# A feed-forward stage on TensorE with its matmuls in another order: the two token halves interleaved, weights shared by neighbours

## What is computed

```python
def reference(x, norm1_gain, w_in, ..., norm2_gain, w_ffn_gate, w_ffn_up, w_ffn_down):
    ...
        h = h + mixed @ w_out[l]
        u = rms_norm(h, norm2_gain[l])
        h = h + (jax.nn.silu(u @ w_ffn_gate[l]) * (u @ w_ffn_up[l])) @ w_ffn_down[l]
    return h
```

## Time and profile before

| | us |
|---|---|
| median of 3 runs | 1255.2 |
| lowest, highest | 1255.13, 1256.24 |
| span of the profiled execution | 1252.1 |
| TensorE busy in it | 1220.7 |
| VectorE, ScalarE, GpSimd busy | 633.8, 377.6, 228.9 |

### The profile page before, as it was taken

How to read it: one execution, slowest core, us unless ns; L and a number is a source line. 1 busy time by engine, 2 the same in 40 slices (tenths; PEclk the granted TensorE clock), 3 DMA queues, 4 the chain that set the end, 5 groups by cost and what they waited for, 6 DMA issues and landing times.

```text
span 1252.1 us, 14986 instructions
## 1 busy us (share of the span) xinstructions
PE 1220.7 (97%) x5840; PEld 1005.0 (80%) x5840; DVE 633.8 (51%) x832; ACT 377.6 (30%) x578; POOL 228.9 (18%) x155
## 2 busy tenths in 40 slices
PE   4999999999999999999999999999999999999998
PEld 4898766678888788778888888888888888888887
DVE  7305576577869795656343334343443425252514
ACT  6314454554545632452212121121212121121110
POOL 6301123342533330241100000000000000101010
PEclk9999999999999999999999999999999999999999
DMA  6101100000001302211101111011111211010003
GB/s 236 50 1 52 34 17 1 18 34 35 18 35 68 148 18 88 85 51 68 68 34 44 56 34 67 34 67 34 58 42 34 66 34 67 34 67 0 0 0 134
DMA packets 20056, 63.47 MB, mean 51 GB/s; under 512 B 3121, under 2 KB 5169, under 8 KB 20017
## 3 DMA queue, kind: packets, MB, share of 16 engines
q1 hardware_dynamic: 20016, 62.94, 14.3%
HBM read 58.74 MB, written 4.19 MB: 50 GB/s over the span
## 4 chain that ended last, share of the span: by engine, by line
PE 88%; DVE 5%; ACT 3%; issue 2%; POOL 1%; DMA 0%; SPq 0%; DVEq 0%; ACTq 0%
PE ps L761 27%; PE ps L763 26%; PE ps L762 26%; PE ps L927 4%; PE ps L888 1%; PE ps L902 1%; PE ps L903 1%; DVE ulo L1030 1%; DVE vlo L1024 1%; POOL D L519 1%; PE ps L953 1%; DVE B L1155 1%; POOL rec L507 0%; DVE M L1188 0%; DMA x<-xT 0%
## 5 line engine op out<-in xcount | busy, mean ns | idle before, releaser
L761 PE MATMUL ps<-u2hi,fhi 128*128 128x512 f32 x704 | 274.6, 390 | 0.9 <-DVE u2lo L1237 0.9
L763 PE MATMUL ps<-u2hi,flo 128*128 128x512 f32 x704 | 273.9, 389 | 0.0
L762 PE MATMUL ps<-u2lo,fhi 128*128 128x512 f32 x704 | 273.9, 389 | 0.0
L533 POOL TENSOR_TENSOR gate<-gate,nrs 128x512 f32<-128x512 f32 x44 | 56.7, 1291 | 612.3 <-ACT gate L739 612.3
L1270 DVE TENSOR_TENSOR h<-ps,h 128x512 f32<-128x512 f32 x176 | 116.9, 689 | 81.0 <-PE ps L763 81.0
L761 PEld LDWEIGHTS ps<-u2hi,fhi 128*128 128x128 f32 x704 | 132.2, 188 | 29.7 <-DVE u2lo L1237 1.4
L763 PEld LDWEIGHTS ps<-u2hi,flo 128*128 128x128 f32 x704 | 132.2, 188 | 27.5
L762 PEld LDWEIGHTS ps<-u2lo,fhi 128*128 128x128 f32 x704 | 132.2, 188 | 27.5 <-issue 0.2
L761 PE MATMUL ps<-hidhi,fhi 128*128 128x512 f32 x352 | 136.9, 389 | 0.0
L762 PE MATMUL ps<-hidlo,fhi 128*128 128x512 f32 x352 | 136.9, 389 | 0.0
L763 PE MATMUL ps<-hidhi,flo 128*128 128x512 f32 x352 | 136.9, 389 | 0.0
(11 more groups left out here) (192 smaller groups left out, 1876.8 us busy)
## 6 DMA issues: line engine op xcount, KB each, us to landing
fraw<-wu SPq DMA_DIRECT2D x22, 512.0 KB, 4.5
fraw<-wg SPq DMA_DIRECT2D x22, 512.0 KB, 3.2
fraw<-wd SPq DMA_DIRECT2D x22, 512.0 KB, 3.8
wraw<-wproj SPq DMA_DIRECT2D x17, 512.0 KB, 3.2
x<-xT SPq DMA_DIRECT2D x8, 512.0 KB, 6.9
h<-xT SPq DMA_DIRECT2D x8, 512.0 KB, 3.8
yT<-h SPq DMA_DIRECT2D x8, 512.0 KB, 2.6
vraw<-wv SPq DMA_DIRECT2D x16, 160.0 KB, 5.7
```

Source lines behind the costliest of these rows:

```text
L533: nc.gpsimd.tensor_tensor(gv, gv, nrs[:, half * HALF:(half + 1) * HALF], ALU.mult)\
L761: nc.tensor.matmul(out, whi_, xhi_, start=first, stop=False)
L762: nc.tensor.matmul(out, whi_, xlo_, start=False, stop=False)
L763: return nc.tensor.matmul(out, wlo_, xhi_, start=False, stop=last)
```

## The change

A new helper `both` takes the place of `three` in `ffn`. For one weight tile it issues the products of both token halves together, six matmuls: high weight by high activation of half 0, then of half 1; high by low of half 0, of half 1; low by high of half 0, of half 1. So each matmul goes to the other bank than the one before it. The loop over halves within p is gone: the two halves' last matmuls follow each other at the end of p, and each raises `s_fmm`. Down issues its groups in twos in the same way. The waits that stood ahead of a half now stand ahead of both and are for the later count: 16i - 2 additions instead of 16i - 3 ahead of p = 0 and 2, both Ln instead of the first ahead of p = 3, two additions at once from q = 2 on. The column sums of the norm stand behind both halves of p = 2. (15 blank lines at the file's head went away too, so line numbers are 15 less above the edit.)

```diff
@@ -967,44 +952,52 @@
                             if m == KT - 1:
                                 mm.then_inc(s_fmm, 1)
 
+            def both(outs, w_hi, w_lo, x_hi, x_lo, first, last):
+
+                for out, v in zip(outs, x_hi):
+                    nc.tensor.matmul(out, w_hi, v, start=first, stop=False)
+                for out, v in zip(outs, x_lo):
+                    nc.tensor.matmul(out, w_hi, v, start=False, stop=False)
+                return [nc.tensor.matmul(out, w_lo, v, start=False, stop=last) for out, v in zip(outs, x_hi)]
+
             def ffn(i, first):
+                halves = [slice(half * HALF, (half + 1) * HALF) for half in range(2)]
                 for p in range(2 if first else 0, 4):
                     pe.wait_ge(s_flo, 6 * i + (p + 1))
-                    for half in range(2):
-                        t = slice(half * HALF, (half + 1) * HALF)
-
-                        if first:
-                            pe.wait_ge(*((s_oadd, 48) if p == 2 else (s_nln, half + 1)))
-                        else:
-                            pe.wait_ge(s_dadd, 16 * i + (2 * p + half) % 4 - 3)
-                        for k in range(KT):
-                            w = slice(k * P, (k + 1) * P)
-                            mm = three(ps[:, ffn_bank(first, p, half), :], fhi[p][:, w], flo[p][:, w], u2hi[:, k, t],
-                                       u2lo[:, k, t], k == 0, k == KT - 1)
+                    if first:
+                        pe.wait_ge(*((s_oadd, 48) if p == 2 else (s_nln, 2)))
+                    else:
+                        pe.wait_ge(s_dadd, 16 * i + (2 * p + 1) % 4 - 3)
+                    for k in range(KT):
+                        w = slice(k * P, (k + 1) * P)
+                        mms = both([ps[:, ffn_bank(first, p, half), :] for half in range(2)], fhi[p][:, w], flo[p][:, w],
+                                   [u2hi[:, k, t] for t in halves], [u2lo[:, k, t] for t in halves], k == 0, k == KT - 1)
+                    for mm in mms:
                         mm.then_inc(s_fmm, 1)
-                        if first and p == 2 and half == 0:
-
-                            pe.wait_ge(s_nacc, KT - 1)
-                            for x2 in range(2):
-                                nc.tensor.matmul(ps[:, (2, 7)[x2], :], ones[:, :], nacc[:, x2 * HALF:(x2 + 1) * HALF],
-                                                 start=True, stop=True).then_inc(s_nss, 1)
+                    if first and p == 2:
+
+                        pe.wait_ge(s_nacc, KT - 1)
+                        for x2 in range(2):
+                            nc.tensor.matmul(ps[:, (2, 7)[x2], :], ones[:, :], nacc[:, x2 * HALF:(x2 + 1) * HALF],
+                                             start=True, stop=True).then_inc(s_nss, 1)
                 for q in range(4):
                     for j in range(2):
                         if q == 0:
                             pe.wait_ge(s_flo, 6 * i + (4 + j + 1))
                             pe.wait_ge(s_hlo, 4 * i + (2 * j + 2))
-                        for b in range(4):
-                            m, half = 2 * q + b // 2, b % 2
+                        for r in range(2):
+                            m = 2 * q + r
                             if j == 0 and q > 1:
-                                pe.wait_ge(s_dadd, 16 * i + (4 * (q - 2) + b + 1))
-                            if j == 0 and q == 1 and b == 0:
+                                pe.wait_ge(s_dadd, 16 * i + (4 * (q - 2) + 2 * r + 2))
+                            if j == 0 and q == 1 and r == 0:
                                 pe.wait_ge(s_hid, 4 * i + 4)
                             w = slice(m * P, (m + 1) * P)
-                            t = slice(half * HALF, (half + 1) * HALF)
-                            mm = three(ps[:, down_bank(first, 4 * q + b), :], fhi[4 + j][:, w], flo[4 + j][:, w],
-                                       hidhi[:, j, t], hidlo[:, j, t], j == 0, j == 1)
+                            mms = both([ps[:, down_bank(first, 4 * q + 2 * r + half), :] for half in range(2)],
+                                       fhi[4 + j][:, w], flo[4 + j][:, w], [hidhi[:, j, t] for t in halves],
+                                       [hidlo[:, j, t] for t in halves], j == 0, j == 1)
                             if j:
-                                mm.then_inc(s_dmm, 1)
+                                for mm in mms:
+                                    mm.then_inc(s_dmm, 1)
 
             ffn(0, True)
             with pe.Fori(1, FT // 2) as i:
```

## The result

The changed kernel took 1265.13 us (median of 6; the kernel before, run beside it, 1256.01). The ratio is 1.0071, with a 95% interval from 1.0048 to 1.0094: slower, by 9 us. The span of its profiled execution, the fastest of the six, is 1261.1 us, 9.0 more than before.

What follows compares the result with a forecast made beforehand. TensorE was taken as the bound, busy 1220.7 of 1252.1 us. Terms 0 + 1.0 + 0.7 + 4.5 + 0.4 = 6.6 us on 1255.2 gave 1261.8 us, 0.5% slower, range 1258.3 to 1267.

Steps and rivals of the forecast that it cites:

- The cadence: TensorE's 128x512 matmuls in the feed-forward part: still 226.7 ns from start to start after the reordering, 0 us change.
- Rival A: Matmuls into the other bank or with loaded weights drop their 13.3 ns: faster, about 1221 us, or 1241; 6%.
- The first pair: Later column sums delay the norm's chain: TensorE stalls 1.6 us for Ln and 2.9 for hidlo, 4.5 us.
- The loop waits: Ten loop passes: stalls of 0.10 us at down's second weight pair and 0.07 at pass start, 1.0 and 0.7 us.
- The tail: End of the kernel: the last groups end closer together, so the last addition comes 0.4 us later.
- last addition at 1255.4: Sign expected in the changed kernel's profile: the time in us of the last addition.
- rival D: TensorE's clock falls to the 1.2 GHz level after the new 2.9 us stall: 1.1 us, or 2; 15%.
- Rival C: Loop waits on computed counts cost 0.3 us each, 20 times: 6 us instead of 1.7, 1266 us; 12%.
- The load ahead of a wait: Weight loads start only when a wait ends, so 0.17 us per restart; pulled past waits, about 5 us in sum.
- The sum's own case: The summed stalls hold, clock fall included: 4.1 to 9.1 us more, 1259.3 to 1264.3 us; 74%.

Runs made afterwards that it cites:

- e3: Changed kernel with the norm's column sums ahead of p = 2, and loop p = 3 and down's q = 3 half by half; 0.9991 of the kernel before.
- e6: Changed kernel with each weight tile's six matmuls reordered: one neighbouring pair shares weights instead of four, banks still alternating; 1268.2 us, one run.
- e1: Changed kernel with the norm's column sums moved ahead of p = 2 of the first pair; 1.0031 of the kernel before.
- e4: Kernel before with one edit, the norm's column sums issued behind both halves of p = 2; 1.0050 of the kernel before.
- e7: Changed kernel with the norm's column sums three quarters into p = 2 of the first pair; 1.0052 of the kernel before.
- e5: Changed kernel with VectorE's two waits ahead of hid and of each addition swapped, the wait for TensorE last; 1.0073 of the kernel before.

## Why the prediction was right, and by how much it was off

- **The cadence: right.** 0 was taken; e3 and e6 show it. Rival A is out, with its rule: by the Trainium skill (TensorE: Matmul & The Clock Gate, Back-to-back issue gap) an isolated warm gap at 512 columns is about 216 ns; no stream here comes below 226.7, with four neighbouring pairs of six sharing weights or with one.
- **The first pair: right.** Forecast 4.5 us in two stalls of 1.6 and 2.9 (the profile's 1.4 and 2.6 are these less the 0.16 us that it does not count, within 0.15). Measured from the N2 restart: the sums come 13.76 us after it instead of 8.30 (5.46 later, forecast 5.44), the second weight pair of down 33.60 instead of 29.10, 4.5 us, and 0.1 more for the restart. e1 removes it, e4 alone makes it, e7 takes the 2.7 us off that its shift says. The chain from nrs to hidlo sets it, link by link as in the rows.
- **The loop waits: the mechanism right, the size wrong.** This is the term that failed: 0.10 + 0.07 us a pass were forecast, 0.43 were measured (0.21 at hidlo, 0.22 at the start of a pass). From the start of the first pass (599.80; before 595.42) to the last matmul's start (1256.58; before 1248.00) it is 656.78 us instead of 652.57: 4.2 us in all, where 1.7 was forecast. The step was "hid starts at 1204.90, S + 0.42". That row is of VectorE's last pass, which is written out with waits on constants. In the loop it is 0.52. The kernel before shows it, in rows that I had and did not use, and the changed kernel's last pass is back at 0.42; both stand under this list. There the wait cost 0.11 us, about the 0.10 of the forecast. e5 shows where the 0.1 comes from in the loop: it goes when the wait for TensorE stands behind the other wait on a computed count and not ahead of it. What the engine does in this time no run shows. The rest of the miss is the 0.01 to 0.04 us by which the stream is slower for a few steps behind each restart.
- **The tail: right.** 0.4 forecast; the last addition starts 0.80 us behind the last matmul's start at 1256.58, 0.42 before. The sign "last addition at 1255.4" did not follow from the sum: 1248.42 + 6.6 is 1255.0, and 1255.4 counts the tail twice. It was 1257.38.
- **The clock: rival D holds, and had too small a chance.** It was given 15% and 1.1 to 2 us. It takes 1.5 to 1.6 us, in five profiles of six. The row I leaned on was a wait of 3.48 us, which seemed longer than mine; but it was the near row. By the Trainium skill (TensorE: Matmul & The Clock Gate, HAM oscillation — how this bites in real kernels) idle gaps between bursts of matmuls put the clock back to its half level. The trace of e4 agrees (0.426 us a step behind the stall), but the page tells it of longer waits that come in every round of a loop; here one shorter stall did it, in most executions and not in all.
- **Rival C** (dearer waits in the loop) was the right place and gave the right reason, waits on computed counts with register steps ahead, but on TensorE; they sit on VectorE. At 0.2 us each, where C had 0.3, it is between forecast and C.
- **The load ahead of a wait.** By the Trainium skill (TensorE: Matmul & The Clock Gate, What happens when you issue a matmul) a load is pulled ahead. By the traces it is ahead by one matmul in the steady stream, and not past a wait: at 646.23 both start together. Keeping the 0.17 us was right.
- **The ranges.** Some of the hit is the range's width. The sum's own case, with 74%, ended at 9.1 us more or 1264.3 us; 9.1 us more was measured, and 1265.13 us lies above it and is caught by the part that C added. That upper end gave the loop at most 3 us, where its own bounds of 0.3 us for each of twenty waits allow 6.

The hid latencies of the third point, first in the loop of the kernel before, at the end of the first half of an up stage (all engines; TensorE's last matmul, then hid: 0.52):

```profile
611.52 0.39 PE L763 MATMUL ps<-u2hi,flo 128*128 128x512 f32 x1
...
612.04 0.69 DVE L1254 TENSOR_TENSOR hid<-ps,gate 128x512 f32<-128x512 f32 x1 [4.84 <-PE ps L763]
```

and in the last pass of the changed kernel, which is written out (0.42):

```profile
1234.48 0.61 PE L961 MATMUL ps<-u2hi,flo 128*128 128x512 f32 x2
...
1234.90 1.29 DVE L1247 TENSOR_TENSOR hid<-ps,gate 128x512 f32<-128x512 f32 x2 [9.59 <-PE ps L961]
```

The sum by measured terms is 4.6 + 4.2 + 0.4 = 9.2 us, as in the edited part, and 1.5 to 1.6 more where the clock falls.

## What to carry to other kernels

When two results that used to be ready one after the other become ready together, the second one's way through the next engine gets longer by one instruction of that engine, and any sum that was put between them moves back by a whole half: look for the wait with the least to spare, not at the engine's busy share. Take latencies from a pass of the same kind, in the loop or out of it, since VectorE's start behind TensorE was 0.1 us later in the loop than in the pass written out. Where two waits stand ahead of an instruction, try both orders and read the latency in each kind of pass: with the late wait last it fell by 0.1 us in the loop and rose by 0.07 in the written-out pass. Interleaving banks and sharing weights between neighbours was no gain by itself here, where each matmul brings its own load and the stream is full.

## What the runs showed that was not expected

The order of two waits on one instruction is worth 0.1 us in the loop when the first is the late one (0.52 and 0.42 us from the matmul's start to VectorE's), and the other way round, 0.42 and 0.50, in the pass written out. The clock falls in most executions behind a stall of 2.5 to 3.2 us of TensorE, stays at 1.2 GHz for 3 to 3.5 us, and costs 1.5 to 1.6 us then. Why it fell in five profiles and not in the sixth stays open: the stalls were alike, and runs without a profile give only their mean clock. It does not belong to the edit alone. Ahead of it, around a wait of 2.2 us for `S` at 434.75 us in the kernel before, the granted clock from 430 to 445 us is 1.00 in the profiles of before and changed and 0.89 in the eight others, though the code there is the same; the sixth profile is one of these two. The five come from three chips; the record names none for the sixth. The 13.3 ns by which a 128x512 matmul is slower than its columns stay unexplained: neither bank nor shared weights change them.
